# Reordering the last scale block in the load queue, and the low weight parts around the gated quarters, in a two-block network on one core

## What is computed

```python
m = silu(c) @ w_mod + b_mod                  # 3 x 2048 columns
shift, scale, gate = split(m, 3)
h = rms_norm(x) * (1 + scale) + shift
u, g = split(h @ w_in, 2)                    # 2048 columns each
pooled[i] = window_mean(u[i], w) - u[i]      # four groups of 512 columns, w = 2, 4, 8, 16
y = einsum(pooled, w_grp) * pool_scale
x = x + gate * ((y * silu(g)) @ w_out)
```

## Time and profile before

| | us |
|---|---|
| median of 3 runs | 1341.62 |
| lowest, highest | 1340.92, 1343.47 |
| the profiled execution | 1341.56 |
| its span | 1339.7 |
| PE busy | 1332.1 |
| DVE busy | 975.6 |
| ACT busy | 735.9 |

### The profile page before, as it was taken

The page is one execution under the profiler, slowest core; times in us unless marked ns, Lnnn a source line. Parts: engine busy times, 40 slices in busy tenths (PEclk is TensorE's granted clock), DMA queues, the critical chain, the costliest instruction groups (busy, mean ns, idle before and its releaser), DMA issues.

```text
span 1339.7 us, 19604 instructions
## 1 busy us (share of the span) xinstructions
PE 1332.1 (99%) x7279; PEld 1124.8 (84%) x7279; DVE 975.6 (73%) x1309; ACT 735.9 (55%) x1096; POOL 142.3 (11%) x233
## 2 busy tenths in 40 slices
PE   9999999999999999999999999999999999999999
PEld 5445999988888888888999988888888888888887
DVE  4558999988679898999677668846667576665552
ACT  2213445555656656556688775465655646555531
POOL 0000012000001000000000100002234224201000
PEclk9999999999999999999999999999999999999999
DMA  9999999875566766586644756656878988877662
GB/s 382 396 416 365 372 347 409 325 252 190 173 234 222 229 228 221 178 272 208 195 141 155 223 185 234 190 188 212 261 227 249 276 251 267 237 222 211 199 197 83
DMA packets 86516, 328.90 MB, mean 245 GB/s; under 512 B 11088, under 2 KB 11488, under 8 KB 81952
## 3 DMA queue, kind: packets, MB, share of 16 engines
q1 hardware_dynamic: 67392, 261.30, 56.9%
q0 software_dynamic: 19040, 66.45, 16.2%
HBM read 305.67 MB, written 24.13 MB: 246 GB/s over the span
## 4 chain that ended last, share of the span: by engine, by line
PE 73%; DMA 12%; DVE 10%; issue 2%; ACT 2%; SPq 0%; POOL 0%; DVEq 0%; ACTq 0%; POOLq 0%
PE acc L838 27%; PE acc L842 14%; PE acc L781 9%; PE acc L782 9%; PE acc L783 9%; DMA mod_ring<-mod_w 7%; DVE w_lo L1784 3%; DMA raw<-weights 3%; PE misc L1094 2%; DMA gate_ring<-weights 2%; DVE mod_ring L1754 1%; DVE gate_ring L1754 1%; DMA l_x<-l_d 1%; PE misc L1084 1%; DVE mod_late L1754 1%
## 5 line engine op out<-in xcount | busy, mean ns | idle before, releaser
L1784 DVE TENSOR_TENSOR w_lo<-raw,w_hi 128x1024 fp32r<-128x1024 f32 x392 | 470.4, 1219 | 166.4 <-ACT w_hi L1258 162.0
L1258 ACT ACTIVATE w_hi<-raw 128x1024 fp32r<-128x1024 f32 x392 | 405.4, 1054 | 309.3 <-DMA raw<-weights 225.7
L838 PE MATMUL acc<-b_op,w_hi 128*128 128x512 f32 x1280 | 324.6, 395 | 0.2 <-DVE vo L1828 0.2
L838 PEld LDWEIGHTS acc<-b_op,w_hi 128*128 128x128 f32 x1280 | 230.1, 189 | 42.3 <-DVE vo L1828 0.4
L842 PEld LDWEIGHTS acc<-b_op,w_lo 128*128 128x128 f32 x1280 | 174.5, 190 | 12.9
L842 PE MATMUL acc<-b_op,w_lo 128*128 128x256 f32 x1280 | 178.3, 282 | 0.0
L781 PE MATMUL acc<-w_hi,b_op 128*128 128x512 f32 x384 | 150.1, 391 | 0.0
L782 PE MATMUL acc<-w_lo,b_op 128*128 128x512 f32 x384 | 149.5, 389 | 0.0
L783 PE MATMUL acc<-w_hi,b_op 128*128 128x512 f32 x384 | 149.4, 389 | 0.0
L838 PE MATMUL acc<-a_op,w_hi 128*128 128x512 f32 x512 | 129.0, 394 | 0.7 <-DVE a_op L1794 0.7
L838 PEld LDWEIGHTS acc<-a_op,w_hi 128*128 128x128 f32 x512 | 92.2, 189 | 17.5 <-ACT w_hi L1258 0.9
(11 more groups left out here) (297 smaller groups left out, 1929.8 us busy)
## 6 DMA issues: line engine op xcount, KB each, us to landing
raw<-weights SPq DMA_DIRECT2D x392, 512.0 KB, 4.7
mod_ring<-mod_w SPq DMA_DIRECT2D x26, 1024.0 KB, 14.7
u_ring<-weights SPq DMA_DIRECT2D x32, 512.0 KB, 14.2
gate_ring<-weights POOLq DMA_DIRECT2D x30, 512.0 KB, 8.5
mod_late<-mod_w SPq DMA_DIRECT2D x6, 1024.0 KB, 7.7
head_d<-head POOLq DMA_DIRECT2D x32, 128.0 KB, 4.1
t<-head_d POOLq DMA_DIRECT2D x32, 128.0 KB, 5.9
p_d<-p_tt POOLq DMA_DIRECT2D x16, 192.0 KB, 5.2
```

The lines of the kernel that those rows point to most:

```text
L838: nc.tensor.matmul(to, w_hi[:, slot, ch], op[:, kt], start=kt == 0, stop=False, skip_group_check=True)
L1258: nc.scalar.activation(w_hi[:, m.c % HL_SLOTS], raw[:, q.c % RAW_SLOTS], ACT.Copy).then_inc(own.up(s_hi), 1)
L1784: nc.vector.tensor_tensor(w_lo[:, slot], raw[:, q.c % RAW_SLOTS], w_hi[:, slot].bitcast(F32), ALU.subtract).then_inc(own.up(s_lo), 1)
```

## The change

Two orders are changed, and no instruction is added or removed.

In SP's queue the last two slices of u are issued as: scale block 14, first half 14, scale block 15, first half 15, second half 14, second half 15. In the order before, both halves of slice 14 stood ahead of scale block 15.

In DVE's queue each gated quarter has one low weight part (41 + j) between the multiplications and `lo_tiles`, and the parts 45 to 48 with their two gate reductions follow after all four quarters. ACT's and PE's queues are as before.

```diff
@@ -531,7 +531,7 @@
-            for kt in range(KT):
+            for kt in range(KT - 2):
                 if kt not in (5, 6):
                     mod_block(scale_at(kt))
...
@@ -546,6 +546,11 @@
+            for kt in (KT - 2, KT - 1):
+                mod_block(scale_at(kt))
+                u_piece(kt, 0)
+            for kt in (KT - 2, KT - 1):
+                u_piece(kt, 1)
...
@@ -1942,9 +1947,9 @@
                 dve.sem_inc(own.also(s_free), 1)
-                lo_parts(Num(N_GRP + 9 + 2 * j), 1)
+                lo_parts(Num(N_GRP + 9 + j), 1)
                 lo_tiles(a_lo[:, 4 * j:4 * j + 4], tiles(z), a_hi[:, 4 * j:4 * j + 4], O_H + 1 + j)
-                lo_parts(Num(N_GRP + 10 + 2 * j), 1)
+            lo_parts(Num(N_GRP + 13), 4)
```

## The result

| | before | after |
|---|---|---|
| median of 20 runs, us | 1341.2 | 1343.8 |
| lowest, highest | 1339.57, 1344.67 | 1340.19, 1346.3 |
| ratio after / before | | 1.0015, 95% interval 1.0009 to 1.0021 |
| span of the profiled execution | 1339.7 | 1342.2 |
| its time | 1341.56 | 1344.01 |

The change makes the kernel 2.0 us slower by the ratio (1.2 to 2.8) and 2.6 us slower by the medians. The forecast was 1.2 us slower, 1342.8. The measured 1343.8 lies in the range (1340.6 to 1345.0).

The account below looks back on a forecast made before the run. PE's queue was taken as the bound: its gaps of 0.65 and 0.84 us go, but 1.65 us of added DVE idle less 0.44 spare starts slab 48 1.2 us later; 1341.56 + 1.2 = 1342.8, range 1340.6 to 1345.0.

Parts of the forecast that it names:

- The forecast case: Whole kernel: slab 48 starts 1.2 us later than before, giving 1342.8; chance 0.60.
- (c): Rival at the gated quarters: load of part 47 held up 6.8 us, DVE 4.75 us late, time 1345.9; chance 0.12.
- the signs of being wrong: Slab 48 before 270.3, load of part 47 over 5 us, or DVE reaching quarter 0 at another time than 238.9.
- the list written down ahead: DVE's steps from quarter 0 at 238.91, priced by start-to-start times, with 1.65 us of added idle time.
- Part 1: Load queue at the end of u: scale block 15 there 1.2 us earlier, saving PE 0.65 us before vo[15].
- Part 2: Gated quarters: slab 42's gap goes, but DVE's added idle time of 1.65 us makes PE wait 2.7 us before slab 48.
- The two idle times: DVE standing 0.64 and 1.0 us before the `lo_tiles` of quarters 2 and 3, for ACT's rounding of z.
- The wait before slab 48: PE ready at 269.25 stands 2.7 us until DVE frees the bank at 271.95.
- rival (e): PE's clock falls to 1.2 GHz for one slab after the 2.7 us gap before slab 48: 1345.6; chance 0.03.
- (a): Rival at the gated quarters: ACT's queue does not bind, DVE has no added idle time, time 1341.1; chance 0.12.
- (b): Rival: DVE also reaches quarter 0 earlier than 238.91 and PE keeps 0.65 + 0.84 us: 1340.1; chance 0.04.
- (d): Rival: no visible effect, 1341.6; first DVE idle time vanishes, second at its lower bound; chance 0.09.

Follow-up runs that it names:

- the bank earlier: Changed kernel with gated_half(0, 0) moved in DVE's queue to behind low part 49 alone; median 1340.00 against 1341.16 for the kernel before, ratio 0.9994.
- both moves: Changed kernel with ACT's queue in DVE's order and gated_half(0, 0) behind part 49 alone; ratios to the kernel before 0.9980, then 0.9987 the second time.
- the queue alone: Kernel before with only the change's new load order in SP's queue, DVE's queue as before; median 1341.26 against 1341.16, ratio 1.0008.
- The run with the wait filled: Changed kernel with five extra unused fp32 products in PE's queue between slabs 47 and 48; median 1344.19 against 1341.68 for the kernel before, ratio 1.0018.
- the reordered queue of ACT: Changed kernel with one high part ahead of each quarter's rounding of z, parts 45 to 48 behind all four; 1341.53 against the kernel before's 1341.16, ratio 1.0007.
- repeat of the kernel before: The kernel before, unchanged, profiled once more in one execution; 1343.70 us.
- low parts alone: Kernel before with only the change's new order in DVE's queue, load queue as before; median 1342.58 against 1341.16, ratio 1.0009.

## Why the prediction was right

**The number.** The forecast case was 1342.8 with bounds of its own, 1342.4 to 1343.5. The measured median of 1343.8 lies above them, and is inside the range only because the range was made wider, for part of (c) and for the scatter of the runs. One of the signs of being wrong came true as well: DVE's chain reached quarter 0 at another time than 238.9. So the mechanism was right and the size of the loss was put too low.

**The bound.** The profiles bear out that PE's queue sets the end. Slab 49's start follows DVE's arrival through the list written down ahead, and where DVE is taken out of the way the spread shrinks from the 4 to 6 us of the changed kernel and the kernel before to 1.4 us (the bank earlier, and both moves the first time) and 1.8 us (both moves the second time).

**Part 1.** The block was taken 1.4 us earlier (1.2 forecast) and PE's gap of 0.65 us went. The gain passed the window products: PE began g at 131.51 against 132.20, 0.69 us earlier, where 0.5 to 0.65 was forecast. The prediction had read the old start as 131.94, so there were 0.4 us to spare behind DVE's low part, not 0.1. The gap of 0.65 us was one execution's: in the five profiles with the old queue it is 0.3 to 0.65 us and g begins at 131.6 to 132.2, and in the nine with the new one there is no gap and g begins at 130.7 to 131.5. The second half of slice 14 was in time. As said, DVE did not come earlier by it, and the queue alone gained nothing.

**Part 2.** DVE's steps came as priced. From quarter 0 to the low part of z of quarter 1 the three profiles of the changed kernel agree with the list within 0.02 us. The two idle times were forecast as 0.64 and 1.0 us. They were 0.31 and 1.06 in the first profile, 0.48 and 1.02 in the second, 0.37 and 0.87 in the third (in the forecast's counting, from start to start, 0.08 more each). Together they put `gated_half(0, 0)` 31.0 to 31.3 us behind quarter 0 instead of 29.6: 1.4 to 1.7 us, for 1.65. The load of part 47 took 3.6 us where 3.7 was taken. The estimate of 3.2 us from the Trainium skill ("DMA: Bandwidth & Descriptors", section "Anatomy of one DMA — SWDGE (gpsimd) path"), whose figures are for transfers that GpSimd issues, was below all the landings of this stretch (3.3 us and more), and the sum was right to go by the rows. The wait before slab 48 was 2.8, 2.8 and 2.6 us, for 2.7. The net loss, once the scatter of DVE's arrival is taken out, was 35.8 - 34.6 = 1.2 us: the forecast. It is the difference between profiles in which the clock stayed full.

**What the sum did not hold.** The measured loss was 2.0 us by the ratio, 0.8 us above the forecast. Two terms were missing or too small. First, DVE's arrival at quarter 0 was taken as fixed at 238.91. It scatters by 2.7 us between executions. Since PE follows it both before and after, this widens the spread more than it moves the difference, but it leaves a gap at slab 42, 0.4 to 0.55 us in the three profiles, which the forecast had at zero. Second, rival (e), the clock, had 0.03. A fall came in 18 of 31 executions. No profile of the changed kernel caught one; in the two profiles that did, it cost 1.6 us and not 2.8, since the clock was back before the slab ended. The mechanism was right and the chance far too small: one gap of 0.84 us at full clock was no evidence about one of 2.7 us. As an estimate from these counts, 1.6 us in 18 of 31 executions instead of 11 of 96 is some 0.75 us more on the mean, which would close the sum. The run with the wait filled does not confirm it, so the 0.8 us are argued and not shown.

**The rivals.** (a) was made on purpose by the reordered queue of ACT: slab 49 stood 0.36 us earlier against quarter 0 than before, where 0.44 was worked out, though the times do not show it (1.0007, 0.9998 to 1.0016). (b) did not come: DVE's arrival with the new queue lies in the scatter of the old one. Its price was too high as well, since a DVE that is 0.65 us earlier frees the bank at 269.65, not by 269.25, and slab 48 would gain 1.1 us and not 1.5. (d) did not come either: the interval of the ratio starts at 1.0009. (c) did not come: no load of part 47 in the three profiles took over 3.8 us.

## What to carry over

Two engines that work through the same parts in lockstep have to be reordered together: moving DVE's list alone left its small step waiting for a rounding that stood, in ACT's list, behind a part that was still loading. When a wait is taken away, look for the first bank or buffer that the same engine frees further down. A list with 0.44 us to spare there turned a gain into a loss, and moving that release ahead of work that nobody yet waited for took back 2.8 us by the ratios. With ACT's list reordered too, the kernel was about 2 us faster than before the change.

## What the hardware showed that was not expected

In this stretch PE's clock fell to its lower level after a single wait of 2.1 us (repeat of the kernel before) and of 2.7 us (low parts alone), was there for 3.4 us, and cost 1.6 us each time. Waits of 2.2 to 2.8 us passed without it in four other profiles. "TensorE: Matmul & The Clock Gate" in the Trainium skill, section "What's actually happening", has the clock gated down by idleness, which these rows bear out. They show as well that nearly the same wait does it in some executions and not in others.

The loads arrive with a scatter that is carried into the rest. ACT began to round part 8, on its landing, between 145.0 and 147.6 in the fourteen profiles, and DVE's arrival at quarter 0 came 92.4 to 93.2 us after it each time. So a lateness of this load was still there over 90 us later, behind a stretch in which the DMA engines are full. What made the load late is not shown. Where PE has slack against DVE's chain, as with both moves, the time hardly shows it.
